# Two output blocks computed together at each hand-over of a two-layer encoder, and ScalarE's squares of x put behind its high halves

## The chip, the cores and the metric

The kernel runs on one core of a Trainium2 chip. The metric is the device time of one execution in microseconds (us), as the median of several executions; for the kernel before it is 2047.44 us over 3 runs.

## What is computed

The reference is a trunk of two layers over 512 positions of 1024 channels, all in float32. Each layer is a half-weighted SwiGLU feed-forward part, a mixer, and a second such part; a final RMSNorm closes it. The even layer's mixer joins differential attention and 2-D neighbourhood attention, the odd layer's joins a gated linear recurrence and latent attention.

```python
for l in range(DEPTH):
    x = x + 0.5 * swiglu(rmsnorm(x, ffn1_norm[l]), ffn1_wg[l], ffn1_wu[l], ffn1_wd[l])
    h = rmsnorm(x, mix_norm[l])
    x = x + even_mixer(h, ...) if l % 2 == 0 else x + odd_mixer(h, ...)
    x = x + 0.5 * swiglu(rmsnorm(x, ffn2_norm[l]), ffn2_wg[l], ffn2_wu[l], ffn2_wd[l])
return rmsnorm(x, final_norm)
```

Here rmsnorm(x, g) is x * rsqrt(mean(x*x) + eps) * g over the channels. What the change touches is the beginning of each of the six parts that follow a norm.

## The kernel before

**Layout.** x stays in SBUF as eight tiles x[:, b, :] of 128 channels by 512 positions. Weights come from HBM in units of 128 x 2048 float32 (1 MB) through two buffers (raw, wh, wl). Every matrix product is made of three matmuls (`three`, L262 on): each factor is split into a high half (rounded to the matmul's format) and a low half (the remainder), and high by high, high by low and low by high are summed in PSUM. For a weight unit, ScalarE makes the high half wh (`split_hi`, L230) and VectorE the low half wl (`split_lo`, L234). For x, ScalarE makes xgh = gain * x (L313) and VectorE xgl = gain * x - xgh (L299).

**The norm.** It is not applied ahead of a product: the product of the gained x is made first, and its result is multiplied by rB, the reciprocal root mean square of each position. For rB, ScalarE squares the eight tiles of x (L322), the first into acc and the others into two buffers sqt in turn; GpSimd adds those seven to acc (`finish_pool`, L333); TensorE multiplies acc by a matrix of ones (`norm_pe`, L337); ScalarE takes the root (L343) and VectorE the reciprocal (L348).

**The hand-overs.** The text counts the norms n = 0 to 6. n = 0 stands at the start, n = 1 between the first feed-forward part and the even mixer, n = 2 between the even mixer and the second feed-forward part, n = 3 between the layers' feed-forward parts, n = 4 ahead of the odd mixer, n = 5 behind it, n = 6 at the end. At each, TensorE finishes eight banks of the old part in turn (`down_last_pe`), and for each tile b VectorE adds the bank to x (L289 in `finish_dve`), ScalarE makes xgh and then the square of the same tile (`finish_act`), and VectorE makes xgl one tile behind. A square from the fourth on waits until GpSimd has taken the one that held its buffer:

```python
if b >= 3:
    act.wait_ge(sq_sum, 7 * n + b - 2)
dst = acc[:, :] if b == 0 else sqt[:, b % 2, :]
nc.scalar.activation(dst, x[:, b, :], ACT.Square).then_inc(sq_done, 1)
```

At n = 2 the low-half buffers of tiles 4 to 7 are still read by the old part (held=4), so their high halves are made at the end (L325).

**What follows on TensorE.** The first weight unit of the new part holds two output blocks of 128 channels (m = 0, 1), each the sum over eight tiles k, 24 matmuls (`block_T`). The first block waits at each k for xgl of tile k (semaphore xg_lo). Behind it stands the matmul of the norm, which waits for all seven of GpSimd's sums (sq_sum), then the second block, then the next unit's two blocks, which wait for that unit's low half (w_lo).

**What follows on ScalarE and VectorE.** Behind the hand-over, ScalarE makes the high half of that next unit, loads the table of the root and takes the root; VectorE makes the unit's low half and then the reciprocal. At n = 1, ScalarE first issues four transfers of tables (`even_load`, L1226 and L1227), and VectorE waits for them (L1360) ahead of the low half.

**The even mixer's first eight blocks** (`even_pe`, L1239 on) alternate between PSUM banks 0 and 1. Behind block i stands the rotation matmul of block i - 1 (`rot_pe`, L654), which reads q32, VectorE's scaled copy (L1375) of it. VectorE finishes the rotation (L1454, L1457, L1460) with GpSimd's and ScalarE's help (L1469, L1356). In this loop ScalarE makes the high half of a later weight unit only behind its step of a rotation, and VectorE makes that unit's low half ahead of the next scaled copy.

The order of the work on each engine is written out by hand; each engine runs its own queue in order.

## Time and profile before

| | |
|---|---|
| median of 3 runs | 2047.44 us (2046.99 to 2049.24) |
| the profiled execution | 2048.65 us, its span 2046.8 us |
| TensorE clock granted, mean | 0.983 of full speed |
| instructions | 23175 |
| matmuls busy | 1944.8 us, 95% of the span |
| VectorE, ScalarE, GpSimd busy | 48%, 34%, 17% |

Engines are PE (TensorE's matmuls), PEld (its weight loads), DVE (VectorE), ACT (ScalarE), POOL (GpSimd) and SP (which issues transfers). "L264" is line 264 of the kernel. Matmuls are pipelined: a matmul of 512 columns is shown with some 390 ns, but the next one starts some 227 ns behind it. A line of the timeline gives its start, its length, the engine, the line, what is written and read, and in brackets how long the engine had been idle and what ended that.

### The profile page before, as it was taken

What the parts mean: (1) busy time and instruction counts of PE and PEld (TensorE: products, weight loads), DVE (VectorE), ACT (ScalarE), POOL (GpSimd) and SP (SyncE); (2) the same over time, 40 slices, a digit from 0 to 9 for tenths busy, and PEclk for the clock granted to TensorE, in tenths of its full rate; (3) what the DMA queues carried; (4) which work ended last, traced back from release to release, by engine and by line L of the source; (5) the groups of instructions that cost most, each with busy time, mean ns of one, the idle gap of its engine ahead of it and who ended that gap; (6) DMA issues with size and microseconds to landing.
All of it is one profiled execution on the core that took longest, in us unless ns stands there. A gap on an engine that the chain in (4) does not pass through costs nothing.

```text
span 2046.8 us, 23175 instructions
## 1 busy us (share of the span) xinstructions
PE 1944.8 (95%) x8888; PEld 1589.3 (78%) x8888; DVE 974.7 (48%) x1026; ACT 705.5 (34%) x932; POOL 348.6 (17%) x290
## 2 busy tenths in 40 slices
PE   6999999997989999999999999999949999999996
PEld 4888888785868888888878888887736878888885
DVE  6334322668778633432254333225887553343223
ACT  4222221436346422221142222213547642222212
POOL 2111100213213211110021111002248421111001
PEclk9999999999989999999999999999969999999998
DMA  4222222212211222222222222223210022222221
GB/s 150 100 102 93 91 103 103 96 63 53 83 42 42 82 103 102 83 102 103 101 84 92 92 102 102 89 97 100 73 62 21 22 83 102 102 85 100 103 102 41
DMA packets 36211, 176.66 MB, mean 86 GB/s; under 512 B 12752, under 2 KB 13136, under 8 KB 15552
## 3 DMA queue, kind: packets, MB, share of 16 engines
q1 hardware_dynamic: 33696, 172.55, 24.0%
q10 hardware_dynamic: 2304, 2.98, 0.4%
q8 instruction: 34, 0.56, 0.1%
q0 software_dynamic: 160, 0.43, 0.1%
q14 instruction: 17, 0.14, 0.0%
HBM read 173.85 MB, written 2.10 MB: 86 GB/s over the span
## 4 chain that ended last, share of the span: by engine, by line
PE 85%; DVE 7%; ACT 3%; POOL 2%; issue 2%; ACTq 0%; DMA 0%; POOLq 0%; DVEq 0%
PE ps L264 28%; PE ps L266 28%; PE ps L265 28%; POOL acc L333 2%; DVE xgl L299 1%; DVE wl L234 1%; DVE small L677 1%; ACT wh L230 1%; PE ps L1105 1%; ACT eA L685 1%; DVE th L1746 1%; PE ps L860 0%; DVE x L289 0%; PE ps L654 0%; DVE rB L348 0%
## 5 line engine op out<-in xcount | busy, mean ns | idle before, releaser
L264 PE MATMUL ps<-xgh,wh 128*128 128x512 f32 x1792 | 709.6, 396 | 27.4 <-DVE xgl L299 25.4
L266 PE MATMUL ps<-xgh,wl 128*128 128x512 f32 x1792 | 698.7, 390 | 0.0
L265 PE MATMUL ps<-xgl,wh 128*128 128x512 f32 x1792 | 698.5, 390 | 0.0
L234 DVE TENSOR_TENSOR wl<-raw,wh 128x2048 fp32r<-128x2048 f32 (+1 forms) x157 | 360.3, 2295 | 540.4 <-ACT wh L230 540.3
L230 ACT ACTIVATE wh<-raw 128x2048 fp32r<-128x2048 f32 (+1 forms) x157 | 297.9, 1898 | 384.1 <-PE ps L266 382.8
L264 PEld LDWEIGHTS ps<-xgh,wh 128*128 128x128 f32 x1792 | 336.8, 188 | 110.4 <-DVE xgl L299 19.5
L265 PEld LDWEIGHTS ps<-xgl,wh 128*128 128x128 f32 x1792 | 337.1, 188 | 71.0 <-issue 3.4
L266 PEld LDWEIGHTS ps<-xgh,wl 128*128 128x128 f32 x1792 | 336.8, 188 | 70.7
L264 PE MATMUL ps<-ah,wh 128*128 (+1 forms) x704 | 273.9, 389 | 0.0
L265 PE MATMUL ps<-al,wh 128*128 (+1 forms) x704 | 273.9, 389 | 0.0
L266 PE MATMUL ps<-ah,wl 128*128 (+1 forms) x704 | 273.9, 389 | 0.0
L483 POOL TENSOR_TENSOR sg<-sg,rB 128x512 f32<-128x512 f32 x88 | 113.6, 1292 | 799.9 <-ACT sg L428 799.8
L432 ACT ACTIVATE ah<-tg 128x512 f32 (+1 forms) x88 | 55.7, 633 | 347.0 <-DVE tg L460 347.0
L333 POOL TENSOR_TENSOR acc<-acc,sqt 128x512 f32<-128x512 f32 x49 | 71.8, 1466 | 578.0 <-ACT sqt L322 572.4
L428 ACT ACTIVATE sg<-tg 128x512 f32<-128x512 f32 x88 | 55.6, 632 | 322.3 <-DVE tg L455 322.3
L460 DVE TENSOR_TENSOR tg<-ps,sg 128x512 f32<-128x512 f32 x88 | 60.8, 691 | 206.2 <-PE ps L266 204.5
L264 PEld LDWEIGHTS ps<-ah,wh 128*128 128x128 f32 x704 | 132.2, 188 | 27.6
L266 PEld LDWEIGHTS ps<-ah,wl 128*128 128x128 f32 x704 | 132.2, 188 | 27.4
L265 PEld LDWEIGHTS ps<-al,wh 128*128 128x128 f32 x704 | 132.2, 188 | 27.3
L455 DVE TENSOR_TENSOR tg<-ps,rB 128x512 f32<-128x512 f32 x88 | 60.5, 688 | 187.2 <-PE ps L266 187.0
L463 DVE TENSOR_TENSOR al<-tg,ah 128x512 f32 (+1 forms) x88 | 60.5, 687 | 14.0 <-ACT ah L432 13.6
L299 DVE SCALAR_TENSOR_TENSOR xgl<-x,gain,xgh 128x512 fp32r<-128x512 f32 x48 | 55.4, 1176 | 2.1 <-ACT xgh L325 1.3
(241 smaller groups left out, 1555.9 us busy)
## 6 DMA issues: line engine op xcount, KB each, us to landing
raw<-in_units SPq DMA_DIRECT2D x161, 1024.0 KB, 4.7
x<-in_xT ACTq DMA_DIRECT2D x8, 256.0 KB, 5.7
outT<-x SPq DMA_DIRECT2D x8, 256.0 KB, 2.1
relb<-in_rpb SPq DMA_DIRECT2D x64, 24.0 KB, 2.1
cosA<-in_rope_a ACTq DMA_DIRECT2D x1, 256.0 KB, 2.6
sinA<-in_rope_a ACTq DMA_DIRECT2D x1, 256.0 KB, 2.9
cosD<-in_rope_d POOLq DMA_DIRECT2D x1, 192.0 KB, 3.1
sinD<-in_rope_d POOLq DMA_DIRECT2D x1, 192.0 KB, 2.7
```

What stands on the lines that cost most here:

```text
L230: nc.scalar.activation(wh[:, c % 2, 0:n], raw[:, c % 2, 0:n], ACT.Copy).then_inc(w_hi, 1)
L234: nc.vector.tensor_tensor(wl[:, c % 2, 0:n], raw[:, c % 2, 0:n], wh[:, c % 2, 0:n].bitcast(F32), ALU.subtract).then_inc(w_lo, 1)
L264: nc.tensor.matmul(dst, lh, rh, start=first, stop=False)
L265: nc.tensor.matmul(dst, lh, rl, start=False, stop=False)
L266: return nc.tensor.matmul(dst, ll, rh, start=False, stop=last)
L299: nc.vector.scalar_tensor_tensor(xgl[:, b, :], x[:, b, :], gain[:, n * KD + b:n * KD + b + 1], xgh[:, b, :].bitcast(F32), ALU.mult, ALU.su ...
L333: nc.gpsimd.tensor_tensor(acc[:, :], acc[:, :], sqt[:, b % 2, :], ALU.add).then_inc(sq_sum, 1)
L432: nc.scalar.activation(ah[:, bass.ds(2 * p + m, 1), :], tg[:, m, :], ACT.Copy).then_inc(a_hi, 1)
L455: nc.vector.tensor_tensor(tg[:, m, :], ps[:, m, :], rB[:, :], ALU.mult).then_inc(tg_done, 1)
L460: nc.vector.tensor_tensor(tg[:, m, :], ps[:, 2 + m, :], sg[:, m, :], ALU.mult).then_inc(a32_done, 1)
L463: nc.vector.tensor_tensor(al[:, bass.ds(2 * p + m, 1), :], tg[:, m, :], ah[:, bass.ds(2 * p + m, 1), :].bitcast(F32), ALU.subtract).then_i ...
L483: nc.gpsimd.tensor_tensor(sg[:, m, :], sg[:, m, :], rB[:, :], ALU.mult).then_inc(s2_done, 1)
```

## The change

Three things are changed. TensorE computes the first unit's two blocks together: for each k it waits for xgl of tile k, then does the three matmuls of block 0 and the three of block 1 (`block_T2`), and the norm's matmul comes behind both. ScalarE makes all eight high halves of x first and then squares the eight tiles (at n = 1 to 5; at n = 0 and n = 6 the old order stands). In the even mixer the eight blocks take four banks in turn (0, 1, 6, 7), and the rotation of block i - 2 stands behind block i.

```diff
--- before.py
+++ after.py
@@ -265,16 +265,26 @@
             nc.tensor.matmul(dst, lh, rl, start=False, stop=False)
             return nc.tensor.matmul(dst, ll, rh, start=False, stop=last)
 
-        def block_T(pe, dst, c, m, width=P, step=256, nt=KD, wait_x=None):
+        def block_T(pe, dst, c, m, width=P, step=256, nt=KD):
 
             s = c % 2
             for k in range(nt):
-                if wait_x is not None:
-                    pe.wait_ge(xg_lo, wait_x + k + 1)
                 o = k * step + m * P
                 mm = three(dst, wh[:, s, o:o + width], wl[:, s, o:o + width],
                            xgh[:, k, :], xgl[:, k, :], k == 0, k == nt - 1)
             return mm
+
+        def block_T2(pe, dsts, c, wait_x):
+
+            s = c % 2
+            for k in range(KD):
+                pe.wait_ge(xg_lo, wait_x + k + 1)
+                for m in range(2):
+                    o = k * 256 + m * P
+                    mm = three(dsts[m], wh[:, s, o:o + P], wl[:, s, o:o + P],
+                               xgh[:, k, :], xgl[:, k, :], k == 0, k == KD - 1)
+                    if k == KD - 1:
+                        mm.then_inc(w_half, 1)
 
         def finish_dve(dve, n, scale, last_unit, held=KD, split=None):
 
@@ -299,6 +309,16 @@
             nc.vector.scalar_tensor_tensor(xgl[:, b, :], x[:, b, :], gain[:, n * KD + b:n * KD + b + 1],
                                            xgh[:, b, :].bitcast(F32), ALU.mult, ALU.subtract).then_inc(xg_lo, 1)
 
+        def square_act(act, n, b):
+            if b == 0 and n:
+                act.wait_ge(ssum_done, n)
+            if b == 1 and n:
+                act.wait_ge(sq_sum, 7 * n)
+            if b >= 3:
+                act.wait_ge(sq_sum, 7 * n + b - 2)
+            dst = acc[:, :] if b == 0 else sqt[:, b % 2, :]
+            nc.scalar.activation(dst, x[:, b, :], ACT.Square).then_inc(sq_done, 1)
+
         def finish_act(act, n, last_unit=None, held=KD, split=None):
             for b in range(KD):
                 if b == KD // 2 and split is not None:
@@ -312,18 +332,15 @@
                         act.wait_ge(w_half, 2 * (last_unit + 1))
                     nc.scalar.activation(xgh[:, b, :], x[:, b, :], ACT.Copy,
                                          scale=gain[:, n * KD + b:n * KD + b + 1]).then_inc(xg_hi, 1)
-                if b == 0 and n:
-                    act.wait_ge(ssum_done, n)
-                if b == 1 and n:
-                    act.wait_ge(sq_sum, 7 * n)
-                if b >= 3:
-                    act.wait_ge(sq_sum, 7 * n + b - 2)
-                dst = acc[:, :] if b == 0 else sqt[:, b % 2, :]
-                nc.scalar.activation(dst, x[:, b, :], ACT.Square).then_inc(sq_done, 1)
+                if n in (0, 6):
+                    square_act(act, n, b)
             for b in range(held, KD):
                 act.wait_ge(w_half, 2 * (last_unit + 1))
                 nc.scalar.activation(xgh[:, b, :], x[:, b, :], ACT.Copy,
                                      scale=gain[:, n * KD + b:n * KD + b + 1]).then_inc(xg_hi, 1)
+            if n not in (0, 6):
+                for b in range(KD):
+                    square_act(act, n, b)
 
         def finish_pool(pool, n):
             for b in range(1, KD):
@@ -355,12 +372,13 @@
             first = isinstance(p, int)
             c0, c1 = B, B + 1
             pe.wait_ge(w_lo, 2 * p + c0 + 1)
-            if not first:
+            if first:
+                block_T2(pe, (ps[:, 0, :], ps[:, 1, :]), c0, 8 * n)
+                norm_pe(pe, n, 4)
+            else:
                 pe.wait_ge(tg_done, 2 * p + 22 * f)
-            for m in range(2):
-                block_T(pe, ps[:, m, :], c0, m, wait_x=8 * n if first and m == 0 else None).then_inc(w_half, 1)
-                if first and m == 0:
-                    norm_pe(pe, n, 4)
+                for m in range(2):
+                    block_T(pe, ps[:, m, :], c0, m).then_inc(w_half, 1)
             pe.wait_ge(w_lo, 2 * p + c1 + 1)
             if not first:
                 pe.wait_ge(a32_done, 2 * p + 22 * f)
@@ -646,6 +664,10 @@
         LAM_INIT = 0.8 - 0.6 * 1.0
         QS = 64 ** -0.5
 
+
+        def qa_bank(i):
+
+            return (0, 1, 6, 7)[i % 4]
 
         def rot_pe(pe, i):
             pe.wait_ge(q32_done, i + 1)
@@ -1237,25 +1259,28 @@
                     sp.dma_start(relb[:, h, j, :], src).then_inc(mask_in, 16)
 
         def even_pe(pe):
-            for i in range(8):
+            pe.wait_ge(w_lo, BE + 1)
+            block_T2(pe, (ps[:, qa_bank(0), :], ps[:, qa_bank(1), :]), BE, 8)
+            norm_pe(pe, 1, 4)
+            pe.wait_ge(even_in, 64)
+            for i in range(2, 8):
                 c = BE + i // 2
                 pe.wait_ge(w_lo, c + 1)
-                if i >= 2:
-                    pe.wait_ge(q32_done, i - 1)
-                block_T(pe, ps[:, i % 2, :], c, i % 2, wait_x=8 if i == 0 else None).then_inc(w_half, 1)
-                if i == 0:
-                    norm_pe(pe, 1, 4)
-                    pe.wait_ge(even_in, 64)
-                else:
-                    rot_pe(pe, i - 1)
-                if i == 1:
+                if i >= 4:
+                    pe.wait_ge(q32_done, i - 3)
+                block_T(pe, ps[:, qa_bank(i), :], c, i % 2).then_inc(w_half, 1)
+                if i == 3:
                     norm_reads_pe(pe)
+                rot_pe(pe, i - 2)
+            rot_pe(pe, 6)
             for v in range(2):
                 c = BE + 4 + v
                 pe.wait_ge(w_lo, c + 1)
                 for t in range(TT):
                     if v == 0 and t == 0:
                         pe.wait_ge(rcol_read, 1)
+                    if v == 0 and t >= 2:
+                        pe.wait_ge(q32_done, t + 5)
                     if v == 1:
                         pe.wait_ge(va_lo, t + 1)
                     mm = block_V(ps[:, 4 + t, 0:256], c, lambda b, k, t=t: b[:, k, t * P:(t + 1) * P], 256, 256)
@@ -1372,7 +1397,7 @@
                 dve.wait_ge(w_half, 2 * c + i % 2 + 1)
                 if i >= 2:
                     dve.wait_ge(qc_done, i - 1)
-                nc.vector.tensor_tensor(q32[:, i % 2, :], ps[:, i % 2, :], rB[:, :], ALU.mult).then_inc(q32_done, 1)
+                nc.vector.tensor_tensor(q32[:, i % 2, :], ps[:, qa_bank(i), :], rB[:, :], ALU.mult).then_inc(q32_done, 1)
                 if i >= 1:
                     qa_dve(dve, i - 1)
                 if i == 3:
@@ -1488,13 +1513,13 @@
                 pe.wait_ge(in_read, i - 3)
             if i in (8, 9):
                 pe.wait_ge(cstd_done, i - 7)
-            block_T(pe, ps[0:rows, i % 4, :], c, m, width=rows,
-                    wait_x=32 if i == 0 else None).then_inc(w_half, 1)
+            block_T(pe, ps[0:rows, i % 4, :], c, m, width=rows).then_inc(w_half, 1)
 
         def odd_pe(pe):
-            odd_block_pe(pe, 0)
+            pe.wait_ge(w_lo, BO + 1)
+            block_T2(pe, (ps[:, 0, :], ps[:, 1, :]), BO, 32)
             norm_pe(pe, 4, 4)
-            for i in range(1, 8):
+            for i in range(2, 8):
                 odd_block_pe(pe, i)
 
             pe.wait_ge(csq_sum, 1)
```

How the queues read before and now, at the two engines concerned; names are tiles, "waits" lists semaphores.

ScalarE at n = 1, behind the last weight unit of the first feed-forward part. Before:

```order
L313 ACTIVATE xgh<-x,gain 128x512 [waits x_new]
L322 ACTIVATE acc<-x 128x512 [waits ssum_done]
L313 ACTIVATE xgh<-x,gain 128x512 [waits x_new]
L322 ACTIVATE sqt<-x 128x512 [waits sq_sum]
L313 ACTIVATE xgh<-x,gain 128x512 [waits x_new]
L322 ACTIVATE sqt<-x 128x512
L313 ACTIVATE xgh<-x,gain 128x512 [waits x_new]
L322 ACTIVATE sqt<-x 128x512 [waits sq_sum]
```

Now:

```order
L333 ACTIVATE xgh<-x,gain 128x512 [waits x_new] x8
L320 ACTIVATE acc<-x 128x512 [waits ssum_done]
L320 ACTIVATE sqt<-x 128x512 [waits sq_sum]
L320 ACTIVATE sqt<-x 128x512
L320 ACTIVATE sqt<-x 128x512 [waits sq_sum] x5
L1248 DMA cosA<-in_rope_a 128x512 [waits x_new]
L1248 DMA sinA<-in_rope_a 128x512
L1248 DMA permA<-in_perm 128x128
L1249 DMA eA<-in_lamvec 128x256
L230 ACTIVATE wh<-raw 128x2048 [waits w_half,raw_in0]
L360 ACT_TABLE_LOAD [waits rstd]
L360 ACTIVATE sqt<-ps,small 128x512 [waits ssum_done]
```

All squares now stand behind the eighth high half; the transfers and the next unit's high half stand behind the last square, as they did.

TensorE at the start of the even mixer's first unit. Before:

```order
L264 MATMUL ps<-xgh,wh 128x512 [waits xg_lo,w_lo]
L265 MATMUL ps<-xgl,wh 128x512
L266 MATMUL ps<-xgh,wl 128x512
L264 MATMUL ps<-xgh,wh 128x512 [waits xg_lo]
L265 MATMUL ps<-xgl,wh 128x512
```

Now:

```order
L264 MATMUL ps<-xgh,wh 128x512 [waits xg_lo,w_lo]
L265 MATMUL ps<-xgl,wh 128x512
L266 MATMUL ps<-xgh,wl 128x512
L264 MATMUL ps<-xgh,wh 128x512
L265 MATMUL ps<-xgl,wh 128x512
L266 MATMUL ps<-xgh,wl 128x512
L264 MATMUL ps<-xgh,wh 128x512 [waits xg_lo]
```

Six matmuls instead of three stand behind each wait, and 48 instead of 24 ahead of the norm's.

TensorE around the first rotations of the even mixer. Before, behind the second block (i = 1):

```order
L654 MATMUL ps<-q,permA 128x512 [waits q32_done]
L632 MATMUL ps<-ones,rB 128x1 [waits rstd]
L632 MATMUL ps<-ones,rB 128x1 x3
L264 MATMUL ps<-xgh,wh 128x512 [waits q32_done,w_lo]
L265 MATMUL ps<-xgl,wh 128x512
```

Now, behind the fourth block (i = 3), where they lead to the fifth; ahead of the third stands no more than the norm's matmul:

```order
L650 MATMUL ps<-ones,rB 128x1 [waits rstd]
L650 MATMUL ps<-ones,rB 128x1 x3
L676 MATMUL ps<-q,permA 128x512 [waits q32_done]
L264 MATMUL ps<-xgh,wh 128x512 [waits q32_done,w_lo]
L265 MATMUL ps<-xgl,wh 128x512
```

The rotation shown last here is the second one; the first stands behind the third block.

## Rows read from the trace of the kernel before

**Rows 1.** Page, busy us, share of the span and instructions by engine.
```profile
PE 1944.8 (95%) x8888; PEld 1589.3 (78%) x8888; DVE 974.7 (48%) x1026; ACT 705.5 (34%) x932; POOL 348.6 (17%) x290
```

**Rows 2.** Waits: engine, line, what ended them: us, times, longest.
```profile
PE ps L264 <- DVE xgl L299: 25.4, 18, 14.6
...
PE ps L337 <- POOL acc L333: 3.9, 5, 3.2
```

**Rows 3.** Timeline of PE at n = 3 (start us, us, engine, line, tiles).
```profile
1047.56 0.39 PE L264 MATMUL ps<-xgh,wh 128*128 128x512 f32 x1
...
1055.99 1.12 PE L337 MATMUL ps<-acc,ones 128*128 128x512 f32 x2 [0.17 <-POOL acc L333]
...
1062.42 0.39 PE L264 MATMUL ps<-xgh,wh 128*128 128x512 f32 x1
```

**Rows 4.** Timeline of DVE at n = 3.
```profile
1043.24 0.69 DVE L289 SCALAR_TENSOR_TENSOR x<-ps,x 128x512 f32<-128x512 f32 x1
1043.84 0.75 DVE L299 SCALAR_TENSOR_TENSOR xgl<-x,gain,xgh 128x512 fp32r<-128x512 f32 x1
...
1045.10 1.19 DVE L299 SCALAR_TENSOR_TENSOR xgl<-x,gain,xgh 128x512 fp32r<-128x512 f32 x1
...
1055.11 2.98 DVE L234 TENSOR_TENSOR wl<-raw,wh 128x2048 fp32r<-128x2048 f32 x1 [0.31 <-ACT wh L230]
```

**Rows 5.** Timeline of ACT at n = 3.
```profile
1052.03 0.72 ACT L313 ACTIVATE xgh<-x,gain 128x512 fp32r<-128x512 f32 x1 [0.46 <-DVE x L289]
1052.66 0.61 ACT L322 ACTIVATE sqt<-x 128x512 f32<-128x512 f32 x1
1053.18 1.90 ACT L230 ACTIVATE wh<-raw 128x2048 fp32r<-128x2048 f32 x1
```

**Rows 6.** Timeline of POOL: the seven sums at n = 3; sums at n = 2.
```profile
1044.27 11.66 POOL L333 TENSOR_TENSOR acc<-acc,sqt 128x512 f32<-128x512 f32 x7 [124.34 <-ACT sqt L322]
...
675.18 1.28 POOL L333 TENSOR_TENSOR acc<-acc,sqt 128x512 f32<-128x512 f32 x1 [1.37 <-ACT sqt L322]
...
683.98 5.61 POOL L333 TENSOR_TENSOR acc<-acc,sqt 128x512 f32<-128x512 f32 x4 [4.10 <-ACT sqt L322]
```

**Rows 7.** Timeline at n = 2: DVE, ACT, PE.
```profile
686.73 0.69 DVE L289 SCALAR_TENSOR_TENSOR x<-ps,x 128x512 f32<-128x512 f32 x1 [1.64 <-PE ps L266]
...
687.99 2.55 ACT L325 ACTIVATE xgh<-x,gain 128x512 fp32r<-128x512 f32 x4
...
699.40 0.39 PE L264 MATMUL ps<-xgh,wh 128*128 128x512 f32 x1
```

**Rows 8.** Timeline at n = 1: ACT's queue, DVE, PE.
```profile
385.74 0.35 ACTq L1226 DMA_DIRECT2D cosA<-in_rope_a  x1
...
390.37 0.29 DVE L1360 TENSOR_TENSOR eA<-eA 128x128 f32<-128x128 f32 x1 [2.42 <-DMA eA<-in_lamvec]
...
390.90 2.28 DVE L234 TENSOR_TENSOR wl<-raw,wh 128x2048 fp32r<-128x2048 f32 x1
...
398.28 1.05 PE L632 MATMUL ps<-ones,rB 1*128 1x1 f32 x8
399.26 0.50 PE L264 MATMUL ps<-xgh,wh 128*128 128x512 f32 x1
```

**Rows 9.** Groups of DVE, 396 to 449 us (busy us, mean ns).
```profile
L1457 DVE TENSOR_TENSOR qs<-qs,qc 128x512 f32<-128x512 f32 x8 | 8.2, 1021 | 0.8
```

**Rows 10.** Stretches: PE, PEld, DVE, ACT, POOL busy; granted clock; DMA.
```profile
1562.00:1568.00 6.00, 5.41 (x13) 4.14 (x14) 2.53 (x4) 1.80 (x6) 2.04 (x2) 0.50 0.00 0
```

**Rows 11.** Timeline of PE behind its idle stretches of 4.08 and 3.21 us.
```profile
1562.59 0.79 PE L264 MATMUL ps<-kdh,qdh 96*128 96x512 f32 x1 [4.08 <-DVE kdl L1783]
...
1567.88 1.08 PE L1105 MATMUL ps<-ident,eD 128*128 128x128 f32 x8
...
2033.54 1.13 PE L337 MATMUL ps<-acc,ones 128*128 128x512 f32 x2 [3.21 <-POOL acc L333]
```

**Rows 12.** Stretches at the end of the kernel.
```profile
2035.00:2037.00 2.00, 0.00 (x0) 0.00 (x0) 1.58 (x1) 0.39 (x1) 0.00 (x0) 0.65 0.00 0
```

## The prediction

> **What bounds the kernel now.** I read the page first: matmuls are busy for 95% of the span, every other engine for under half [rows 1]. So only what makes TensorE wait, or slows its clock, moves the end. The list of waits then tells which waits are the change's: 25.4 us for xgl at the starts of the parts, and 3.9 us for GpSimd's sums ahead of the norm's matmul [rows 2]. So some 29 us at most lie where the change works, of which one 14.6 us wait is for the very first tile, before the kernel has anything to compute. That leaves 10.8 us for xgl.
>
> The timeline of one hand-over shows how that comes about; I take n = 3, since n = 4 and n = 5 look the same. TensorE starts the first block at 1047.56, starts the norm's matmul at 1055.99, and starts the next unit at 1062.42 [rows 3]. Between 1047.56 and 1062.42 lie 48 matmuls, which at 227 ns each are 10.9 us, and the norm's, about 0.9 us as its place among them shows; the other 3 us are stalls. VectorE's xgl takes 0.75 us while GpSimd is idle, 1.19 once it sums [rows 4], and so the tiles come each 1.7 us instead of each 1.26. The norm's matmul starts as the last sum ends (1044.27 + 11.66 = 1055.93) [rows 3, 6]. So before the change xgl and the sums arrive almost together, and neither costs much.
>
> **The change, part by part.** Counts of matmuls, squares and sums stay; only their order moves.
>
> *Gain: xgl.* With the squares behind the high halves GpSimd is idle while xgl is made, so a tile takes 1.26 us (1043.84 to 1045.10) [rows 4]. Tile 7 of x is then added at 1043.24 + 5 x 1.26 = 1049.54, until 1050.2. TensorE needs a new tile only each 6 x 0.227 = 1.36 us. The xgl stall goes: both blocks run through, from 1047.56 to 1058.44.
>
> *Loss: the sums.* The first sum now waits for the second square. The last high half starts at 1050.25; the first square 0.63 us behind it, the second 0.52 behind that (spacings of ScalarE) [rows 5], which ends at 1052.02. Then come seven sums. One takes 1.28 us alone, and four in a row took 5.61 [rows 6], which is a spacing of about 1.43. So the fifth ends at 1059.08 and the seventh at 1061.94. TensorE reaches the norm's matmul at 1058.44 and stands there: 3.5 us idle. The stall has moved from xgl to the sums.
>
> *Loss: what stands behind the squares.* The eighth square needs the buffer that the fifth sum frees, so it starts at 1059.1 and the next unit's high half at 1059.63, until 1061.53 (1.90 us) [rows 5]. Its low half starts at 1061.55 but must wait for GpSimd: in rows 4 the same instruction began at 1055.11, sums ran until 1055.93 [rows 6], and it ended at 1058.09, 2.16 us behind them. So it ends at 1061.94 + 2.16 = 1064.10, and the next unit starts at 1064.15 instead of 1062.42 [rows 3]: **+1.7 us**, three times (n = 3, 4, 5), +5.1. Behind that, the reciprocal and the scaling have a whole unit of TensorE's time (10.9 us) as cover; nothing is added.
>
> The Trainium skill (SBUF — State Buffer, "SBUF: two separate sides") says that VectorE instructions with two SBUF inputs and GpSimd take their shared port pair by an exclusive lock held for the whole instruction. The trace agrees (0.75 us against 1.19), and by this rule alone the change looks like a gain, since it separates the two users; the rule prices the 0.44 us per tile and says nothing of the chain of sums.
>
> *n = 2.* Here the sums were spread over the old part's banks and ended long before. Now ScalarE starts the four late high halves when tile 7 is added (686.73 + 0.69), which take 2.55 us [rows 7], to 690.0; the second square ends at 691.05, the seventh sum at 691.1 + 9.87 = 700.97, the low half at 703.13; the next unit starts at 703.2 instead of 699.40 [rows 7]: **+3.8 us**.
>
> *n = 1.* The same schedule, with the fifth sum's end about 392.2 (x is added 666.85 us earlier than at n = 3). Now the four transfers stand behind the eighth square. Before, the first was issued at 385.74 and VectorE started at 390.37, 4.6 us later [rows 8]; so it now starts at 396.8, and 0.53 us later (390.37 to 390.90) the low half, until 399.6. The third block starts at 399.65 instead of 399.26: +0.4. But before, a rotation (0.86 us) and the reads of the norm (1.0 us: 398.28 to 399.26) [rows 8] had been done by then and are now still to do: +1.9. And the loop is tighter. From a rotation's end to the next unit's low half there are VectorE's 0.69 and 1.02 us (the former length is that of any scaled copy from PSUM [rows 4, 9]), ScalarE's 0.63 and 1.90, VectorE's 2.28: 6.5, some 6.8 with the hand-overs. TensorE brings one block and one rotation as cover, 5.44 + 0.86 = 6.3, where before it had two blocks. So I expect about 0.4 us of wait at the seventh block, and about 1.3 and 0.8 at the last two rotations, which need scaled copies that VectorE makes behind that low half. Sum **+5.0 us**.
>
> *n = 0.* No order of squares changes here. The blocks end sooner, but the next unit's low half depends on VectorE's small setup work, as before: **0**.
>
> *n = 6:* unchanged. Order sum: 5.1 + 3.8 + 5.0 = 13.9 us.
>
> *The clock.* The idle stretches are now in one piece. After 4.08 us without matmuls TensorE ran at half its clock: twelve matmuls from 1562.59 to 1567.88, 5.29 us instead of 12 x 0.227 = 2.72 [rows 10, 11], 2.6 us lost. At the end of the kernel, 3.21 us idle and then only the norm's matmul were followed by a fall of the clock as well: 0.65 granted in the next stretch [rows 11, 12]. Each of n = 1 to 5 will have just that: 3.4 us idle, the norm's matmul, another 1 us idle (n = 1: 3 us). At n = 0 there will be some 4 to 5 us of idle. No row shows six such places, so the cost lies between nothing (no fall) and 6 x 2.6 = 15.6 us; I take 2.0 us each, 12 us, near the upper row since it is the same kind of gap, and less than it since the norm's matmul breaks the gap.
>
> The Trainium skill (TensorE: Matmul & The Clock Gate, "HAM oscillation — how this bites in real kernels") says that a long idle gap puts the clock back to half, and that a loop with one such wait per group of matmuls pays for it every time. It speaks against this change: it collects scattered waits into one. By it the sum would carry the clock term in full; without it the sum would end at 13.9 us.
>
> **Sum.** Against the profiled execution (2048.65 us, span 2046.8): 13.9 + 12 = 25.9, so 2074.5. That execution lies 1.2 us above the median, so against the median of 2047.44 I forecast **2073 us**.
>
> **Rivals.**
> (a) *The clock stays up.* For it: the gap of 3.21 us by itself showed no slow matmul, and at n = 3 to 5 I expect 3.4. Against: rows 12. It gives 2047.4 + 13.9 = 2061. Chance 0.16.
> (b) *Faster: the sums keep up.* If GpSimd summed in no more than about 0.9 us each, the seventh sum would be there when TensorE comes (6.4 us after the first started), no stall would remain, and each of five hand-overs would lose its 3 us: 2047 - 15 = 2032. It decides at 0.9 us per sum; the shortest in the trace is 1.28 alone [rows 6], and ScalarE needs 0.52 per square, so it isn't the brake. This is where the rule on the shared ports (the Trainium skill, SBUF — State Buffer) would lead if the sums cost nothing once they no longer meet VectorE; the rows put them at 1.28 us even then. Chance 0.03.
> (c) *No difference.* TensorE waits for the sums, but the low half is not late, and n = 1 costs nothing: the norm's matmul would start at 1062 and the next unit about 1062.9, +0.5 at each place, with the clock up: 2050. It needs ScalarE to pass the eighth square, which a queue in order doesn't do. Chance 0.03.
>
> **Numbers.** My forecast (order and clock) has 0.78. The range takes in rival (a) with 2 to 3 us for the errors of the schedule, hence 2058, and above my forecast 7 us, for the clock's upper end and a longer loop at n = 1, hence 2080. About 0.2% (4 us) is what a measurement of this kernel tells from no change. Slower by more than that: 0.78 + 0.16 = 0.94; within it 0.03; faster 0.03.
>
> **What the profile of the changed kernel would show.** TensorE's wait for xgl is down to the first tile; its wait for acc (the norm's matmul) has grown from 3.9 us to some 17 at n = 1 to 5, over 3 us each. xgl takes 0.75 us throughout. The seven sums at n = 3 take about 9.9 us and start 1.8 us behind the last addition to x. The low half of the next unit ends last, about 23 us behind the first addition, and TensorE waits for it 1 us (n = 2 to 5), 3 us or more (n = 1). The granted clock shows 0.5 behind each hand-over, matmuls spaced by 0.43 us. I am wrong if the sums end before TensorE reaches them, if no place shows a lower clock, or if the next unit at n = 3 starts less than 21.4 us behind the first addition.

## The result, and the profile after

The changed kernel takes 2073.54 us (median of 4 runs, 2073.22 to 2075.76). The kernel before took 2048.34 us beside it (4 runs, 2046.99 to 2049.37). The ratio is 1.012, with a 95% interval of 1.0105 to 1.0136: the change costs 25 us. The prediction was 2073.0, in a range of 2058 to 2080.

The first lines to read are the page's busy times and the list of TensorE's waits. Page of the changed kernel (busy us, share, instructions):

```profile
span 2071.9 us, 23171 instructions
PE 1956.0 (94%) x8888; PEld 1599.6 (77%) x8888; DVE 958.8 (46%) x1026; ACT 708.7 (34%) x932; POOL 341.1 (16%) x290
```

Waits of TensorE in the changed kernel (us in total, times, longest):

```profile
PE ps L264 <- DVE wl L234: 36.8, 5, 27.5
PE ps L354 <- POOL acc L350: 20.4, 6, 3.6
PE ps L264 <- DVE xgl L309: 15.0, 1, 15.0
```

Against [rows 2], the wait for xgl has gone except for the very first tile: 25.4 us in 18 waits became 15.0 in one. The wait for GpSimd's sums has grown from 3.9 to 20.4 us, and the low half wl, which was late once (27.8 us, inside the odd mixer), is now late five times. The trade is as forecast: 10.4 us less wait at xgl, and 16.5 + 9.0 = 25.5 more at the other two. The same matmuls are busy 11 us longer than in [rows 1]. That is the clock, whose mean fell from 0.983 to 0.974.

One hand-over shows the order of events; I take n = 3, to set beside [rows 3 to 6]. Timeline of the changed kernel at n = 3, VectorE and ScalarE:

```profile
1052.60 1.28 DVE L299 SCALAR_TENSOR_TENSOR x<-ps,x 128x512 f32<-128x512 f32 x2
1056.01 0.68 DVE L299 SCALAR_TENSOR_TENSOR x<-ps,x 128x512 f32<-128x512 f32 x1
1056.61 0.74 DVE L309 SCALAR_TENSOR_TENSOR xgl<-x,gain,xgh 128x512 fp32r<-128x512 f32 x1
1057.27 0.68 DVE L299 SCALAR_TENSOR_TENSOR x<-ps,x 128x512 f32<-128x512 f32 x1
...
1061.77 0.72 ACT L333 ACTIVATE xgh<-x,gain 128x512 fp32r<-128x512 f32 x1 [0.54 <-DVE x L299]
1062.40 0.62 ACT L320 ACTIVATE acc<-x 128x512 f32<-128x512 f32 x1
1062.92 1.14 ACT L320 ACTIVATE sqt<-x 128x512 f32<-128x512 f32 x2
...
1070.67 0.63 ACT L320 ACTIVATE sqt<-x 128x512 f32<-128x512 f32 x1 [0.79 <-POOL acc L350]
1071.21 1.89 ACT L230 ACTIVATE wh<-raw 128x2048 fp32r<-128x2048 f32 x1
```

GpSimd's sums, VectorE's low half of the next unit, and TensorE, at the same hand-over:

```profile
1063.62 9.84 POOL L350 TENSOR_TENSOR acc<-acc,sqt 128x512 f32<-128x512 f32 x7 [132.17 <-ACT sqt L320]
1073.13 2.47 DVE L234 TENSOR_TENSOR wl<-raw,wh 128x2048 fp32r<-128x2048 f32 x1 [9.85 <-ACT wh L230]
1059.07 0.39 PE L264 MATMUL ps<-xgh,wh 128*128 128x512 f32 x1
...
1073.51 1.20 PE L354 MATMUL ps<-acc,ones 128*128 128x512 f32 x2 [3.40 <-POOL acc L350]
1075.66 0.80 PE L264 MATMUL ps<-xgh,wh 128*128 128x512 f32 x1 [0.95 <-DVE wl L234]
```

Read it as a chain. Additions to x come each 1.26 us (1056.01 to 1057.27), since xgl takes 0.74 us with GpSimd idle. The squares begin only at 1062.40. From the fourth on each stands some 0.8 us for a buffer that a sum frees, so ScalarE goes at GpSimd's pace. The seven sums take 9.84 us. TensorE has been through with its 48 matmuls at 1073.51 - 3.40 = 1070.11 and stands until 1073.51; the next unit's high half begins behind the last square, and its low half lets the next unit start at 1075.66. That is 1075.66 - 1052.60 = 23.06 us behind the first addition, where it was 1062.42 - 1041.09 = 21.33 before [rows 3]. The first addition at n = 3 in the kernel before:

```profile
1041.09 1.28 DVE L289 SCALAR_TENSOR_TENSOR x<-ps,x 128x512 f32<-128x512 f32 x2
```

The low half also shows the meeting of VectorE and GpSimd: it starts at 1073.13, the last sum ends at 1073.46, and the low half ends 2.14 us behind it, having taken 2.47 us instead of the 2.29 that it takes alone.

Behind the stall the clock falls. Stretches of the changed kernel (PE, PEld, DVE, ACT, POOL busy; granted clock; DMA share, GB/s):

```profile
1058.00:1060.00 2.00, 2.00 (x11) 1.65 (x10) 2.00 (x4) 1.44 (x2) 0.00 (x0) 1.00 0.00 0
1076.00:1081.00 5.00, 5.00 (x13) 3.85 (x13) 4.16 (x3) 2.11 (x4) 0.67 (x1) 0.50 0.59 210
1081.00:1083.00 2.00, 2.00 (x10) 1.65 (x9) 0.30 (x1) 1.66 (x1) 1.88 (x2) 0.94 0.00 0
```

The granted clock is 1.00 while the blocks run and 0.50 from 1076 to 1081, that is 1.2 instead of 2.4 GHz. The Trainium skill's page "TensorE: Matmul & The Clock Gate", section "HAM oscillation — how this bites in real kernels", has it that a wait repeated in each round puts the clock down each time; by that rule the loss comes back at every hand-over, and the trace agrees at all of n = 1 to 5.

### The profile page after: what moved, and what is told of

The parts are those of the page before. It is cut to its first block, busy times and chain, and to the rows that moved or that the text cites. A ratio compares the mean times of both kernels' runs of the same rounds, so it can differ in the third digit from the quotient of the medians.

```text
span 2071.9 us, 23171 instructions
## 1 busy us (share of the span) xinstructions
PE 1956.0 (94%) x8888; PEld 1599.6 (77%) x8888; DVE 958.8 (46%) x1026; ACT 708.7 (34%) x932; POOL 341.1 (16%) x290
## 3 DMA queue, kind: packets, MB, share of 16 engines
q10 hardware_dynamic: 2304, 2.98, 0.4%
## 4 chain that ended last, share of the span: by engine, by line
PE 82%; DVE 8%; ACT 4%; POOL 2%; issue 2%; ACTq 0%; DMA 0%; POOLq 0%; DVEq 0%
PE ps L264 27%; PE ps L266 27%; PE ps L265 27%; POOL acc L350 2%; DVE wl L234 1%; DVE xgl L309 1%; ACT wh L230 1%; DVE x L299 1%; DVE small L699 1%; ACT eA L707 1%; PE ps L1127 1%; DVE th L1771 1%; PE ps L882 0%; PE ps L676 0%; ACT xgh L333 0%
## 5 line engine op out<-in xcount | busy, mean ns | idle before, releaser
L350 POOL TENSOR_TENSOR acc<-acc,sqt 128x512 f32<-128x512 f32 x49 | 64.4, 1315 | 621.3 <-ACT sqt L320 615.3
L266 PEld LDWEIGHTS ps<-ah,wl 128*128 128x128 f32 x704 | 132.1, 188 | 27.3
L309 DVE SCALAR_TENSOR_TENSOR xgl<-x,gain,xgh 128x512 fp32r<-128x512 f32 x48 | 42.2, 894 | 2.3 <-ACT xgh L339 1.0
```

The costliest lines, as they stand in the source:

```text
L266: return nc.tensor.matmul(dst, ll, rh, start=False, stop=last)
L309: nc.vector.scalar_tensor_tensor(xgl[:, b, :], x[:, b, :], gain[:, n * KD + b:n * KD + b + 1], xgh[:, b, :].bitcast(F32), ALU.mult, ALU.su ...
L350: nc.gpsimd.tensor_tensor(acc[:, :], acc[:, :], sqt[:, b % 2, :], ALU.add).then_inc(sq_sum, 1)
```

## The experiments

Of the three things changed, the joint blocks and the late squares can be had one without the other, and the first two kernels take one each. The even mixer's four banks and later rotations go with the joint blocks in every kernel here; they were not timed apart.

**The joint blocks alone.** The old order of squares stands again:

```diff
-                if n in (0, 6):
-                    square_act(act, n, b)
+                square_act(act, n, b)
...
-            if n not in (0, 6):
-                for b in range(KD):
-                    square_act(act, n, b)
```

> The change with the squares in their old places (each behind the high half of its tile), so that only the joint blocks and the even mixer's four banks remain. Theory S (the loss is the chain of late squares and sums): the sums end near 1055.9 at n = 3 as before, ahead of the joint blocks' end at 1058.4; the next unit starts at once behind the norm's matmul, near 1059.4 instead of 1062.4, so 3 us less at n = 3, 4, 5, about 1 at n = 2, about 3 at n = 1, and about 2 us lost to the clock at n = 0: 2048 - 9 = 2039 (2036 to 2042). Rival J (the joint blocks or the later rotations themselves cost): 2050 or more.

Measured: 2037.83 us, ratio 0.9934 (0.9915 to 0.9953). Timeline at n = 3:

```profile
1044.13 11.71 POOL L346 TENSOR_TENSOR acc<-acc,sqt 128x512 f32<-128x512 f32 x7 [124.34 <-ACT sqt L320]
1058.30 1.02 PE L350 MATMUL ps<-acc,ones 128*128 128x512 f32 x2
1058.75 0.80 PE L264 MATMUL ps<-xgh,wh 128*128 128x512 f32 x1
```

No idle time stands before the norm's matmul, and the next unit follows at once. The sums are slow here too (11.71 us for seven), but they start 3.2 us behind the first addition to x (1040.95) and end at 1055.84, 2.5 us early. So the joint blocks are a gain by themselves, even though xgl is still slowed to 1.18 us a tile: six matmuls behind each tile leave TensorE enough to do. At n = 1, where the rotations come later too, less of it is kept: the third block starts 5.9 us sooner behind the first addition than before (19.09 against 25.01), but the first value unit behind the eight blocks only 2.8 us sooner (59.99 against 62.79), with the first rotation and the norm's reads to be done in between and 0.63 us of wait at a rotation. A price is paid at n = 0, where TensorE stands 3.83 us before the second unit (below).

**The late squares alone.** The kernel before, with this in `finish_act`:

```diff
-                square_act(act, n, b)
+                if n in (0, 6):
+                    square_act(act, n, b)
...
+            if n not in (0, 6):
+                for b in range(KD):
+                    square_act(act, n, b)
```

> The kernel before with the squares behind the eight high halves at n = 1 to 5, and nothing else. Theory S: the norm's matmul stands behind 24 matmuls instead of 48, reaches its place near 1053 at n = 3 and waits for the sums until 1062, some 9 us; then 24 matmuls of the second block follow, 5.4 us, so the next unit starts near 1068.5 instead of 1062.4. 6 us or more at each of five places and 2 us of clock each: 2048 + 42 = 2090 (2082 to 2095). Rival J: below 2070, since what costs in the change is then missing here.

Measured: 2092.38 us, ratio 1.0205 (1.0185 to 1.0225). TensorE at n = 3, and a stretch around it:

```profile
1079.00 2.07 PE L344 MATMUL ps<-acc,ones 128*128 128x512 f32 x2 [8.71 <-POOL acc L340]
...
1078.00:1080.00 2.00, 1.00 (x1) 0.50 (x2) 1.37 (x1) 1.88 (x2) 0.94 (x1) 0.50 0.00 0
```

With one block of cover instead of two the same sums cost 8.71 us, 5.3 more than in the changed kernel: the 24 matmuls of a block (24 x 0.227 = 5.4 us). The norm's matmul runs at half the clock. So the loss is in the late squares, and the joint blocks hide part of it. In ratios to the kernel before, the joint blocks give 0.66%, the late squares cost 2.05%, and both together cost 1.2%.

**Order and clock apart.** The changed kernel, with matmuls of no use where TensorE would stand (14 before and 2 behind the norm's matmul, 14 and 14 at n = 1, 18 behind it at n = 0). The feed-forward parts are shown; the two mixers have the like:

```diff
+        def filler_pe(pe, n, count):
+
+            for k in range(count):
+                nc.tensor.matmul(ps[:, 5, :], xgh[:, 0, 0:P], xgh[:, k % KD, :], start=True, stop=True)
...
                 block_T2(pe, (ps[:, 0, :], ps[:, 1, :]), c0, 8 * n)
+                filler_pe(pe, n, 14 if n else 0)
                 norm_pe(pe, n, 4)
+                filler_pe(pe, n, 2 if n else 18)
```

> The changed kernel with matmuls that nothing reads, into a PSUM bank that is free, where TensorE would stand idle: 14 ahead of the norm's matmul and 2 behind it at n = 1 to 5 (14 behind it at n = 1), 18 behind it at n = 0. The waits for sums and low half stay. If the clock's fall costs some 2 us at each of six places, the time is 2073.5 - 10 = 2063 (2060 to 2066), and the granted clock stays at full speed near the hand-overs. If the clock costs nothing there (rival: the whole loss is waiting), it is 2073 or above.

Measured: 2062.56 us, ratio 1.0057 (1.0038 to 1.0076). Timeline and one stretch at n = 3:

```profile
1066.72 3.33 PE L355 MATMUL ps<-xgh 128*128 128x512 f32 x14
1070.35 1.12 PE L359 MATMUL ps<-acc,ones 128*128 128x512 f32 x2 [0.29 <-POOL acc L350]
1072.50 0.49 PE L264 MATMUL ps<-xgh,wh 128*128 128x512 f32 x1 [0.55 <-DVE wl L234]
...
1070.00:1073.00 3.00, 2.15 (x7) 1.14 (x7) 3.00 (x2) 2.67 (x3) 0.29 (x1) 1.00 0.00 0
```

The stall is filled, and the clock stays at 1.00. The next unit starts 1072.50 - 1049.38 = 23.12 us behind the first addition, so the sums come no sooner than in the changed kernel. The kernel with useless work is 11 us faster than the same kernel without it. So of the 25 us about 11 are clock, and 14.4 are order (the span, 2061.2 against 2046.8). The two ratios, each to runs of the kernel before taken beside it, stand 0.63% or 13 us apart, so the split holds to some 2 us.

**Which late thing binds: the sums or the low half.** Here the high half of the next unit (with the four transfers at n = 1) is put ahead of the squares, so the low half is early and the sums are later. Shown is where it is called; the lines that pass it in, and take it from its old place, are left out:

```diff
+            if early is not None:
+                early()
             if n not in (0, 6):
                 for b in range(KD):
                     square_act(act, n, b)
```

> The changed kernel with the high half of the next unit (and at n = 1 the four transfers) ahead of the eight squares. Theory S: the low half is then early, but squares and sums start 1.9 us later, and VectorE's low half holds GpSimd's sums up once by some 2 us; the norm's matmul becomes the last wait, near 1065, so nothing is gained and 1 to 2 us are lost at each place: 2080 (2076 to 2085). Rival Q (what ends last is the place of the high half behind the squares, the sums alone would be hidden): 1.1 us less at n = 2 to 5 and 3 less at n = 1, 2066.

Measured: 2083.19 us, ratio 1.0162 (1.0142 to 1.0181), 10 us slower than the changed kernel. Timeline at n = 3:

```profile
1067.23 1.90 ACT L230 ACTIVATE wh<-raw 128x2048 fp32r<-128x2048 f32 x1
1069.17 2.29 DVE L234 TENSOR_TENSOR wl<-raw,wh 128x2048 fp32r<-128x2048 f32 x1 [1.05 <-ACT wh L230]
1070.25 10.85 POOL L352 TENSOR_TENSOR acc<-acc,sqt 128x512 f32<-128x512 f32 x7 [133.98 <-ACT sqt L320]
1081.15 2.08 PE L356 MATMUL ps<-acc,ones 128*128 128x512 f32 x2 [6.21 <-POOL acc L352]
1082.24 1.42 PE L264 MATMUL ps<-xgh,wh 128*128 128x512 f32 x1
```

The low half is ready at 1071.46 and nobody waits for it, but the sums start 1.8 us later and take 1.0 us longer, since the first of them meets the low half. TensorE stands 6.21 us, 2.8 more than the 3.40 of the changed kernel. The next unit starts 1082.24 - 1057.44 = 24.80 us behind the first addition, 1.7 later than in the changed kernel. So the chain of sums is what binds first; the theory that the late low half sets the loss falls.

**The sums made short.** The changed kernel, with each sum on 64 of its 512 columns at n = 1 to 5. This leaves out most of the sum of squares; every wait and instruction stays.

```diff
-                nc.gpsimd.tensor_tensor(acc[:, :], acc[:, :], sqt[:, b % 2, :], ALU.add).then_inc(sq_sum, 1)
+                w = 64 if 1 <= n <= 5 else SEQ
+                nc.gpsimd.tensor_tensor(acc[:, 0:w], acc[:, 0:w], sqt[:, b % 2, 0:w], ALU.add).then_inc(sq_sum, 1)
```

> The changed kernel, with GpSimd's sums at n = 1 to 5 made on 64 of the 512 columns, so the chain of sums is short while every wait and every instruction stays; the output leaves out most of the sum of squares there. Theory S (TensorE stands at the norm's matmul because seven sums, 1.4 us each, begin only behind the eighth high half): the squares then come each 0.5 us, the 3.4 us idle at the norm's matmul is gone at n = 1 to 5, the next unit is no longer late, there is no half-clock stretch behind these hand-overs: 2 to 6 us faster than before, about 2044 us, ratio 0.997. Rival (the late place of the squares in ScalarE's queue is itself what costs, through the next unit's high half): TensorE still waits about 1 us for the next unit and the gain stops at 2053 us or above, ratio 1.002.

Measured: 2043.56 us (2039.25 to 2047.61, 9 runs), ratio 0.9967 (0.9955 to 0.9979). Timeline at n = 3, and TensorE at n = 1:

```profile
1056.09 0.32 POOL L351 TENSOR_TENSOR acc<-acc,sqt 128x64 f32<-128x64 f32 x1 [132.17 <-ACT sqt L320]
...
1059.29 0.32 POOL L351 TENSOR_TENSOR acc<-acc,sqt 128x64 f32<-128x64 f32 x1 [0.23 <-ACT sqt L320]
1062.43 1.02 PE L355 MATMUL ps<-acc,ones 128*128 128x512 f32 x2
1063.39 0.50 PE L264 MATMUL ps<-xgh,wh 128*128 128x512 f32 x1
...
397.05 0.47 PE L264 MATMUL ps<-xgh,wh 128*128 128x512 f32 x1 [2.68 <-DVE wl L234]
```

A sum now takes 0.32 us; the seven are done 3.52 us after the first began instead of 9.84, and at n = 1 to 5 no norm's matmul waits. The late place of the squares is thus no loss against the kernel before when the sums are short. It is still one against the joint blocks alone, by some 6 us: the next unit is half a microsecond late at n = 3 (1063.39 - 1045.08 = 18.31 us behind the first addition, where the joint blocks alone have 1058.75 - 1040.95 = 17.80), and n = 1, with the transfers behind the squares, keeps a stall of 2.68 us against 0.72. One part of the expectation did miss: it had the clock up behind all of n = 1 to 5, but behind n = 1 it fell once more, for 3.4 us. Even with sums this short, then, the late squares buy nothing that the joint blocks have not already.

**Late squares at n = 3, 4 and 5 only.**

```diff
-                if n in (0, 6):
+                if n in (0, 1, 2, 6):
...
-            if n not in (0, 6):
+            if n not in (0, 1, 2, 6):
```

> The changed kernel with the late squares at n = 3, 4 and 5 only; n = 1 and 2 have the old order. If the loss by late squares is local to each hand-over, n = 3 to 5 cost what they cost in the changed kernel: against the joint blocks alone the sum of three hand-overs, 3 x 7 = 21 us at most and 3 x 5 = 15 at least, so about 2056 us (2052 to 2060), ratio 1.0035, with three idle stretches of 3.4 us ahead of the norm's matmul and none at n = 1 and 2. Rival (n = 1, with its loop of rotations, and n = 2, with its held buffers, cost most of it, as the prediction's sum had it: 8.8 of 13.9 us of order): 2048 us or less.

Measured: 2056.94 us (2056.11 to 2061.89, 5 runs), ratio 1.0041 (1.0028 to 1.0054). TensorE's wait for the sums, its timeline at n = 2 and n = 3, and the stretches behind both:

```profile
PE ps L354 <- POOL acc L350: 13.4, 4, 3.4
...
698.00 1.02 PE L354 MATMUL ps<-acc,ones 128*128 128x512 f32 x2
1061.49 1.12 PE L354 MATMUL ps<-acc,ones 128*128 128x512 f32 x2 [3.39 <-POOL acc L350]
...
1064.00:1069.00 5.00, 5.00 (x13) 3.89 (x13) 4.14 (x3) 2.03 (x4) 0.68 (x1) 0.50 0.59 210
698.00:703.00 5.00, 5.00 (x22) 3.77 (x21) 3.23 (x1) 1.97 (x2) 0.00 (x0) 1.00 0.30 125
```

The loss is local: three stalls of 3.39 us with a fallen clock at them (the fourth wait is the one of 3.20 us at n = 6, which every kernel has), and none at n = 1 and 2, where the old order stands. In ratios, the way from the joint blocks alone to the whole change is 1.012 - 0.9934 = 1.86%. Of it n = 3 to 5 have 1.0041 - 0.9934 = 1.07% (7.3 us each), and n = 1 and 2 the other 0.79% (8.1 us each). That last figure is loose, since the runs of this kernel spread from 2056.11 to 2061.89 us. In the profiled executions of the joint blocks alone and of the whole change, the stretches from one hand-over's first addition to the next differ by 4.6 us at n = 1, 6.7 at n = 2, and 7.6, 6.7 and 7.8 at n = 3, 4 and 5. At n = 1 it is 8.3 us up to the first value unit (68.32 against 59.99), of which the mixer gives 3.7 back: it has 10.2 us less of half clock in the changed kernel. The rival, that n = 1 and 2 cost most of it, wanted 2048 us or less and falls.

**A version that beats both.** The joint blocks with the old order of squares, and the small setup work of the start moved behind the first pair of units (calls moved from the top of the program into the first feed-forward part, on both engines):

```diff
             pair(0, True)
+            if f == 0:
+                setup_dve(dve)
...
-            setup_dve(dve)
```

> The joint blocks and four banks with the old order of squares, and the small setup work of VectorE and ScalarE at the kernel's start moved behind the first weight pair of the first feed-forward part. Theory: the wait of 3.8 us ahead of the second unit at n = 0 is VectorE's low half standing behind that setup work, so it goes, and nothing else changes: 4 to 5 us below the joint blocks alone, so about 2034 us (2031 to 2037), ratio to before about 0.993. Rival (the gap at n = 0 is the transfer of that unit or VectorE's backlog of low halves of x, not the setup): the wait stays, the time is that of the joint blocks alone, 2037 to 2039 us.

Measured: 2031.0 us (2029.67 to 2032.67, 5 runs), ratio 0.9911 (0.9897 to 0.9924): 18 us below the kernel before. VectorE and TensorE at the start, first in the joint blocks alone:

```profile
25.53 0.16 DVE L625 TENSOR_SCALAR small<-cvec 128x8 f32<-128x8 f32 x1
...
30.20 0.17 DVE L640 TENSOR_SCALAR small<-small 128x8 f32<-128x8 f32 x1
30.40 2.29 DVE L234 TENSOR_TENSOR wl<-raw,wh 128x2048 fp32r<-128x2048 f32 x1
...
32.75 0.79 PE L264 MATMUL ps<-xgh,wh 128*128 128x512 f32 x1 [3.83 <-DVE wl L234]
```

and with the setup moved:

```profile
25.40 2.28 DVE L234 TENSOR_TENSOR wl<-raw,wh 128x2048 fp32r<-128x2048 f32 x1
...
28.16 1.02 PE L350 MATMUL ps<-acc,ones 128*128 128x512 f32 x2
28.61 0.80 PE L264 MATMUL ps<-xgh,wh 128*128 128x512 f32 x1
```

A row of instructions of 0.17 us each held the low half back by 5 us, and TensorE with it. The old second block, run behind the norm's matmul, had covered that; the joint blocks run 24 matmuls earlier and lay it bare. With the setup out of the way the first addition of n = 1 comes 375.88 - 370.76 = 5.1 us sooner. That is the edit's own gain, at the upper end of the 4 to 5 us expected. The medians stand 6.8 us apart and the ratios 0.23%, 4.7 us; the spans of the profiled executions, 2037.3 and 2028.6, stand 8.7 apart. Of these, 3.4 us lie in the even mixer, where two half-clock stretches of the joint blocks alone, one of them of 6.8 us from 469 us on, are missing in this kernel. I don't count those as the edit's own. So 2031.0 us, at the low end of the range expected, owes something to the clock in the mixers.

## Why the prediction was right

**The terms of order**, against the kernel with the filled stalls, whose clock doesn't fall at n = 0 to 5 (inside the mixers it does, as in all kernels here). Each figure is the growth of the span between two fixed points, the additions to x of successive hand-overs, in the profiled executions:

| place | forecast | filled kernel minus before | changed minus filled (clock) |
|---|---|---|---|
| n = 0 | 0 | 0.1 | 2.0 |
| n = 1 | 5.0 | 4.1 | -0.2 |
| n = 2 | 3.8 | 4.1 | 1.5 |
| n = 3, 4, 5 | 1.7 each | 1.9, 2.1, 1.9 | 2.6, 1.4, 2.8 |
| n = 6 | 0 | 0.2 | 0.7 |
| sum | 13.9 | 14.4 | 10.7 |

- *Gain at xgl*: right. A tile each 1.26 us, TensorE's blocks without a wait.
- *The sums*: right to a tenth. Forecast from [rows 6]: seven sums in 9.87 us and 3.5 us of idle; measured 9.84 and 3.40. The spacing of 1.43 us was read off four sums that had run with a square beside each, and that is what the seven did (squares at 1069.25 and 1070.67 in the timeline of n = 3).
- *Behind the squares*: right. The next unit was forecast 23.06 us behind the first addition, and came 23.06 behind.
- *n = 2*: 16.5 us from the last addition to x to the next unit in the forecast, 709.22 - 692.62 = 16.6 measured.
- *n = 1*: somewhat high, 5.0 us for 4.1; its parts as written add up to 4.8. Transfers and low half came nearly as forecast (the third block 402.04 - 376.26 = 25.78 us behind the first addition, forecast 25.4), but of the 2.5 us of waits in the loop of rotations only 0.64 us came in the changed kernel and 0.63 in the filled one, each at a single rotation. The step "there are VectorE's 0.69 and 1.02 us" used too long a duration: 1.02 us is the mean of an addition that has GpSimd at work beside it, and with the rotations one block later it runs alone, in 0.69 us, ahead of the three low halves inside the loop. That is 0.33 us less for each wait; why the rest of the waits stayed away was not traced. Groups of VectorE in the changed kernel from 396 to 458 us, and the first instance; compare [rows 9]:

```profile
L1482 DVE TENSOR_TENSOR qs<-qs,qc 128x512 f32<-128x512 f32 x8 | 7.1, 884 | 0.8
...
411.04 0.69 DVE L1482 TENSOR_TENSOR qs<-qs,qc 128x512 f32<-128x512 f32 x1
```

- *n = 0*: the order cost nothing, as forecast; the 3.6 us of idle stand where the second block ran before.

**The clock** (at n = 0, 0.3 of the 2.0 us lies ahead of the first sum and is no clock): 12 us forecast, 10.7 by the spans and 11.0 by the medians. "2.0 us each" at six places was a choice between 0 and 2.6, and the places are less alike than that, from -0.2 to 2.8. They add up to 10.0, and 0.7 comes at n = 6, where nothing was forecast: the norm's matmul there takes 2.08 us in the changed kernel and 1.32 in the filled one. So the mechanism was right, but that the total came within 1 us of the measured one is partly luck: the order was put 0.5 us too low and the clock 1.3 too high. At n = 3 and 5 the fall comes behind the norm's matmul and the next unit pays 2.6 to 2.8 us, the full price of [rows 11]. At n = 2 and 4 it comes before, and the norm's matmul itself runs slowly, with less left for the unit: 1.5 and 1.4 us. Timeline of the changed kernel at n = 4:

```profile
1441.02 2.07 PE L354 MATMUL ps<-acc,ones 128*128 128x512 f32 x2 [3.40 <-POOL acc L350]
1443.17 0.80 PE L264 MATMUL ps<-xgh,wh 128*128 128x512 f32 x1
```

At n = 1 the unit pays, and the even mixer gives as much back. From the first addition to the first value unit behind the eight blocks it is 62.79 us before, 66.90 in the filled kernel and 68.32 in the changed one: 4.1 us of order, as in the table, and 1.4 of clock. From there to n = 2 the changed kernel is 1.65 us shorter than both others. It has 17.1 us of half clock there, in stretches of 3.4 and 13.7; the filled one has 23.9 (6.8, 3.4 and 13.7), and the kernel before 20.5 (3.4, and 17.1 from 588 us on). Why those stretches differ isn't known, so the -0.2 says nothing of the price of the fall at n = 1. So rival (a), the clock staying up, was wrong about this kernel, and its 2061 us is what the filled one measured (2062.56).

**The rivals on the other side.** "Faster: the sums keep up" put the deciding point at 0.9 us per sum. With sums of 0.32 us the kernel was faster than before, by 0.33%, not by the 15 us of that rival: from n = 3 to n = 6 it did gain the 3 us per hand-over of that rival (2.9, 3.1 and 2.9), but at n = 2 only 0.7. At n = 0, where it keeps the stall, it lost 1.8. At n = 1 it lost 2.9: 0.8 up to the first value unit, since transfers and low half stand behind the squares, and the rest in the mixer, where this kernel has 27.3 us of half clock against 20.5 before. "No difference" needed the low half to pass the squares; the kernel that makes it pass them is slower still, since the sums then start later.

## What to carry to other kernels

When work is moved behind a batch, ask who drains it: here eight squares of 0.5 us feed seven sums of 1.4 us, and a chain that had run under the batch now starts at its end. Two edits that share a purpose should be timed apart: one of this pair gains 0.7% and the other costs 1.9% on top of it. And a stall on TensorE is priced with what its clock does behind it: here the later work cost 14 us and the slow matmuls behind the stalls another 11.

## What the runs showed that I had not expected

- Useless matmuls made a kernel faster. 3.33 us of them at each stall, ending 0.3 us before the norm's matmul, kept the granted clock at 1.00, and took 11 us off.
- Nearly the same gap, 3.40 us of idle (3.61 at n = 2) and then the norm's matmul, showed its fall of the clock at two different places: ahead of the norm's matmul at n = 2 and n = 4 (2.07 us for it), at its end or behind it at n = 1, n = 3 and n = 5 (1.12, 1.20 and 1.12 us). What sets the place was not tried.
- Half-clock stretches inside the mixers come and go between kernels whose instructions there are the same: 6.8 us at 469 us with the joint blocks alone, nothing there with the setup moved. Executions of one kernel differ as well: with late squares at n = 3 to 5 they took 2056.11 to 2061.89 us, at mean granted clocks of 0.980 to 0.975. This limits how well two kernels' spans can be compared outside the edited places to some 2 to 4 us. The main steps, of 10 us and more, stand clear of that; the 7 us from the joint blocks to the moved setup and the 6 us between the joint blocks and the short sums do so only through what their timelines show at the edited places.
- A low half of 2.29 us took 2.47 when it began 0.33 us ahead of the end of a sum, and ended 2.14 us behind that sum. In the kernel before, the same instruction began 0.82 us ahead of a sum's end, took 2.98 us and ended 2.16 us behind it [rows 4, 6]. So its end goes by the end of the sum and not by its own start: it was held until GpSimd was done. The Trainium skill's page "SBUF — State Buffer", section "SBUF: two separate sides", says that the shared ports are locked for a whole instruction and the other engine is blocked, and these rows agree, but for 0.13 to 0.15 us: behind the sum the low half needed that much less than the 2.29 us that it takes alone.
